# A bias of the attention scores: added by one-hot matmuls in TensorE instead of by a table spread through DRAM

## The reference

```
q, k, v, fz = split(h @ w_in)              # fz: one column for each head
q, k = rms_norm(q, q_g), rms_norm(k, k_g)  # per head
c = cumsum(log_sigmoid(fz + fgate_b))      # over the tokens, one row for each head
for i in range(2):                         # blocks of 128 queries
    logits = q_i @ k[:hi].T * 64 ** -0.5 + c[lo:hi, None] - c[None, :hi]
    probs = softmax(where(causal, logits, -inf))
    out_i = probs @ v[:hi]
x = x + out @ w_out
```

## Time and profile before

| | |
|---|---|
| median of 3 runs | 2485.47 us (2482.64 to 2490.33) |
| the profiled execution | 2485.47 us |
| its span | 2483.8 us |
| granted clock of TensorE, mean | 0.977 |
| busy: TensorE, VectorE, ScalarE, GpSimd | 95%, 66%, 47%, 40% |
| HBM read | 383.46 MB, 155 GB/s over the span |

### The profile page before, as it was taken

How to read it: one execution, slowest core, us unless ns; L and a number is a source line. 1 busy time by engine, 2 the same in 40 slices (tenths; PEclk the granted TensorE clock), 3 DMA queues, 4 the chain that set the end, 5 groups by cost and what they waited for, 6 DMA issues and landing times.

```text
span 2483.8 us, 51333 instructions
## 1 busy us (share of the span) xinstructions
PE 2363.2 (95%) x18282; PEld 2160.6 (87%) x18282; DVE 1642.6 (66%) x3051; ACT 1160.6 (47%) x1603; POOL 1003.5 (40%) x950
## 2 busy tenths in 40 slices
PE   6789998999999999998999989999999999889989
PEld 6779998999988888896899989998888888889987
DVE  5651899577788855435249967778886551334985
ACT  5434544333444455447444433334444454664444
POOL 5516797543333100014578854333320004654430
PEclk9889999999999999999999999999999999999999
DMA  4314555555555566643356545555556664444545
GB/s 144 104 41 139 160 180 155 164 160 160 159 167 165 167 191 193 193 144 111 106 158 184 180 145 158 163 161 162 168 162 185 194 194 131 129 127 135 169 152 152
DMA packets 108198, 385.72 MB, mean 155 GB/s; under 512 B 12464, under 2 KB 14800, under 8 KB 107728
## 3 DMA queue, kind: packets, MB, share of 16 engines
q1 hardware_dynamic: 104400, 379.13, 50.5%
q10 hardware_dynamic: 3712, 5.44, 0.7%
HBM read 383.46 MB, written 1.06 MB: 155 GB/s over the span
## 4 chain that ended last, share of the span: by engine, by line
PE 67%; POOL 12%; issue 10%; DVE 6%; ACT 2%; DVEq 1%; DMA 0%; POOLq 0%; ACTq 0%
POOL w_lo L366 12%; PE bank L1593 10%; PE bank L1595 10%; PE bank L1594 10%; PE bank L1504 9%; PE bank L1505 9%; PE bank L1507 9%; PE bank L1767 4%; DVE big L1416 2%; DVE big L1422 1%; DVE w_lo L871 1%; PE bank L1473 1%; DVE big L906 1%; PE bank L1510 0%; PE bank L1666 0%
## 5 line engine op out<-in xcount | busy, mean ns | idle before, releaser
L468 ACT ACTIVATE w_hi<-ring 128x1024 fp32r<-128x1024 f32 x719 | 758.3, 1057 | 793.1 <-PE bank L1595 422.7
L366 POOL TENSOR_TENSOR w_lo<-ring,w_hi 128x1024 fp32r<-128x1024 f32 x281 | 705.3, 2526 | 917.3 <-ACT w_hi L468 916.5
L1504 PE MATMUL bank<-x_hi,w_hi 128*128 128x256 f32 x3328 | 959.7, 289 | 40.3 <-ACT x_hi L481 16.8
L1505 PE MATMUL bank<-x_hi,w_lo 128*128 128x256 f32 x3328 | 947.0, 285 | 0.0
L1507 PE MATMUL bank<-x_lo,w_hi 128*128 128x256 f32 x3256 | 925.7, 284 | 0.0
L871 DVE TENSOR_TENSOR w_lo<-ring,w_hi 128x1024 fp32r<-128x1024 f32 x438 | 538.2, 1229 | 262.3 <-ACT w_hi L468 255.3
L1504 PEld LDWEIGHTS bank<-x_hi,w_hi 128*128 128x128 f32 x3328 | 645.5, 194 | 54.6 <-issue 24.8
L1505 PEld LDWEIGHTS bank<-x_hi,w_lo 128*128 128x128 f32 x3328 | 645.8, 194 | 0.0
L1507 PEld LDWEIGHTS bank<-x_lo,w_hi 128*128 128x128 f32 x3256 | 629.8, 193 | 0.0
L1593 PE MATMUL bank<-w_hi,x_hi 128*128 128x512 f32 x1112 | 440.4, 396 | 5.9 <-DVE x_lo L878 5.9
L1595 PE MATMUL bank<-w_lo,x_hi 128*128 128x512 f32 x1112 | 434.3, 391 | 0.0
(11 more groups left out here) (252 smaller groups left out, 2015.0 us busy)
## 6 DMA issues: line engine op xcount, KB each, us to landing
ring<-u_dram SPq DMA_DIRECT2D x256, 512.0 KB, 3.7
ring<-v_dram SPq DMA_DIRECT2D x256, 512.0 KB, 4.1
ring<-up_dram SPq DMA_DIRECT2D x44, 512.0 KB, 3.6
ring<-wq_dram SPq DMA_DIRECT2D x32, 512.0 KB, 3.7
ring<-sb_in_dram SPq DMA_DIRECT2D x31, 512.0 KB, 3.8
ring<-od_in_dram SPq DMA_DIRECT2D x25, 512.0 KB, 3.7
ring<-down_dram SPq DMA_DIRECT2D x22, 512.0 KB, 3.6
ring<-ev_in_dram SPq DMA_DIRECT2D x21, 512.0 KB, 3.8
```

Source lines behind the costliest of these rows:

```text
L366: pool.tensor_tensor(w_lo[:, k % RING, :], ring[:, k % RING, :], w_hi[:, k % RING, :].bitcast(F32), ALU.subtract).then_inc(g["lo_pool"], 1)
L468: A(w_hi[:, k % RING, :], ring[:, k % RING, :], ACT.Copy).then_inc(g["w_hi_done"], 1)
L1504: mm(dst, hi[:, rows[c]], xh[:, c, :], start=(c == 0), stop=False)
L1505: mm(dst, lo[:, rows[c]], xh[:, c, :], start=False, stop=False)
```

## The change

The write to DRAM, the spread, the table `fx_tab` and `mask_rows` are taken out. VectorE's masks read the plain causal mask. TensorE adds the bias in PSUM: after the two score matmuls of a block it runs two more that accumulate on them. Their weights are 16 rows of the identity's column `at + h`, repeated over 128 columns, and the moving operand is the 16 bias rows at partition `at` (0 or 64); the product is head h's bias row on all partitions. Before the loop TensorE waits for the bias rows. In VectorE, `head_norm` now runs over all eight blocks in one go, and the wait for the causal mask stands ahead of the loop.

```diff
@@ -175,7 +175,6 @@
         o_v = carve(TB * D)
         o_z = [carve(T) for _ in range(6)]
         causal = carve(3 * P)
-        fx_tab = carve(FH * 3 * P)
         fx_s, fx_p, fx_pt = ([carve(3 * P) for _ in range(4)] for _ in range(3))
         fx_max = carve(4 * 2)
         fx_sum, fx_inv = carve(2 * FH), carve(2 * FH)
@@ -220,8 +219,6 @@
         assert f_at + FC * T <= 27904
 
 
-        rows_dram = nc.dram_tensor("rows_dram", (FH, T), F32).ap()
-
         names = """x_loaded ev_tables_loaded tables_loaded keys_loaded od_tables_loaded sb_tables_loaded stored
             consts
             pieces_used units_out w_hi_done lo_pool lo_dve x_hi_done x_lo_done ax_hi ax_lo
@@ -233,7 +230,7 @@
             ev_chunk_sums ev_states ev_o ev_o_out ev_o_sq ev_o_sum ev_o_root ev_y
             conv_input conv_step taps_laid conv_mixed ln_sum ln_centred ln_sq ln_var ln_root ln_normed ev_ya
             od_z_in od_z_log od_bias_ready od_sq od_sum od_log od_root od_qk_ready od_sel
-            fox_rows_out fox_rows_spread fox_score fox_masked fox_exped fox_turned fox_pt_act fox_pt_dve fox_mixed fox_scaled fox_back
+            fox_score fox_masked fox_exped fox_turned fox_pt_act fox_pt_dve fox_mixed fox_scaled fox_back
             at_score at_masked at_exped at_prob at_turned at_pt at_mixed at_y
             sb_sq sb_sum sb_log sb_root sb_qk_ready sgu_mean sgu_root sgu_v_ready sgu_w_ready
             sgu_mixed sgu_y merged_out merged ff_silu ff_z ff_gated ff_tap""".split()
@@ -749,13 +746,6 @@
                 for s in SUM_GROUPS[j]:
                     A(o_sq[:, s * 512:(s + 1) * 512], o_qk[:, s * 512:(s + 1) * 512], ACT.Square).then_inc(g["od_sq"], 1)
                 unit(token_major(o_v, D, j), view=lambda s: b3(s, TB))
-                if j == 0:
-                    act.wait_ge(g["od_bias_ready"], 1)
-                    act.dma_start(rows_dram, o_z[5][0:FH, :]).then_inc(g["fox_rows_out"], 16)
-                if j == 1:
-                    act.wait_ge(g["fox_rows_out"], 16)
-                    act.dma_start(fx_tab.rearrange("p (h t) -> p h t", h=FH)[:, :, P:3 * P],
-                                  rows_dram.partition_broadcast(P)).then_inc(g["fox_rows_spread"], 16)
                 roots([(o_n[:, s * 512:(s + 1) * 512], bank[4 + s % 4][:, :]) for s in SUM_GROUPS[j]], HD,
                       "od_log", "od_root", 3 * j, "od_sum")
             highs(n[0] + 3)
@@ -1251,23 +1241,13 @@
                 settle()
                 V.tensor_tensor_scan(o_z[5], o_z[0], o_z[4], 0.0, ALU.mult, ALU.add).then_inc(g["od_bias_ready"], 1)
 
-            def mask_rows():
-
-                dve.wait_ge(g["od_sel"], 1)
-                dve.wait_ge(g["fox_rows_spread"], 16)
-                tab = fx_tab.rearrange("p (h c t) -> p h c t", h=FH, c=3)
-                below = causal[:, 0:P].rearrange("p (o t) -> p o t", o=1).to_broadcast([P, FH, P])
-                for dst, src in ((0, 1), (2, 2)):
-                    step(V.tensor_tensor(tab[:, :, dst], tab[:, :, src], below, ALU.add))
-
             def fox():
 
                 def mask(h):
                     S, top = fx_s[h % 4], fx_max[:, (h % 4) * 2:(h % 4) * 2 + 2]
-                    tab = fx_tab[:, h * 3 * P:(h + 1) * 3 * P]
                     dve.wait_ge(g["fox_score"], h + 1)
                     for b, cols in enumerate((slice(0, P), slice(P, 3 * P))):
-                        last = V.tensor_tensor_reduce(S[:, cols], bank[h % 4][:, cols], tab[:, cols], -1.0, -NEG_BIG,
+                        last = V.tensor_tensor_reduce(S[:, cols], bank[h % 4][:, cols], causal[:, cols], -1.0, -NEG_BIG,
                                                       ALU.add, ALU.min, top[:, b:b + 1])
                     last.then_inc(g["fox_masked"], 1)
 
@@ -1292,7 +1272,7 @@
                         V.tensor_tensor(x_lo[:, c], bank[(4, 0)[half] + j % 2][:, :], x_hi[:, c].bitcast(F32),
                                         ALU.subtract).then_inc(g["x_lo_done"], 1)
 
-                settle()
+                dve.wait_ge(g["od_sel"], 1)
                 for j in range(FH // 2):
                     mask(2 * j)
                     if j:
@@ -1306,9 +1286,9 @@
                 low_half(1)
                 xs[0] += 1
 
-            def head_norm(first, count, raw, dst, gain, root, ready):
-
-                for s in range(first, count):
+            def head_norm(count, raw, dst, gain, root, ready):
+
+                for s in range(count):
                     v = dst[:, s * 512:(s + 1) * 512]
                     dve.wait_ge(g[root], s + 1)
                     V.scalar_tensor_tensor(v, raw[:, s * 512:(s + 1) * 512], gain(s), v, ALU.mult, ALU.mult).then_inc(g[ready], 1)
@@ -1348,10 +1328,8 @@
             for k in range(12):
                 low(starts["od_in_b"] + k)
             log_sigmoid_rows()
-            of_qk = lambda s: qk_gain[:, 0:1] if s < 4 else qk_gain[:, 1:2]
-            head_norm(0, 6, o_qk, o_n, of_qk, "od_root", "od_qk_ready")
-            mask_rows()
-            head_norm(6, 8, o_qk, o_n, of_qk, "od_root", "od_qk_ready")
+            head_norm(8, o_qk, o_n, lambda s: qk_gain[:, 0:1] if s < 4 else qk_gain[:, 1:2],
+                      "od_root", "od_qk_ready")
             fox()
             u[0] += 13
             n[0] += 25
@@ -1363,7 +1341,7 @@
             norm(G_MIX2)
             step(V.tensor_scalar(nsink[:, :], sinks[:, :], -1.0, None, ALU.mult))
             dve.wait_ge(g["sb_tables_loaded"], 80)
-            head_norm(0, 3, s_qk, s_n, lambda s: qk_gain[:, 2:3] if s < 2 else qk_gain[:, 3:4],
+            head_norm(3, s_qk, s_n, lambda s: qk_gain[:, 2:3] if s < 2 else qk_gain[:, 3:4],
                       "sb_root", "sb_qk_ready")
             dve.wait_ge(g["units_out"], u[0] + 8)
             for tb in range(TB):
@@ -1832,8 +1810,12 @@
                     for lo, b, keys in ((0, 0, P), (P, 1, 2 * P)):
                         for h in (2 * j, 2 * j + 1):
                             at = 64 * (h % 2)
-                            last = mm(bank[h % 4][:, lo:lo + keys], qk[at:at + 64, j, b * P:(b + 1) * P],
-                                      qk[at:at + 64, 8 + j, 0:keys], start=True, stop=True)
+                            mm(bank[h % 4][:, lo:lo + keys], qk[at:at + 64, j, b * P:(b + 1) * P], qk[at:at + 64, 8 + j, 0:keys],
+                               start=True, stop=False)
+                        for h in (2 * j, 2 * j + 1):
+                            at = 64 * (h % 2)
+                            pick = ident[at:at + FH, at + h:at + h + 1].to_broadcast([FH, P])
+                            last = mm(bank[h % 4][:, lo:lo + keys], pick, o_z[5][at:at + FH, 0:keys], start=False, stop=True)
                             if b:
                                 last.then_inc(g["fox_score"], 1)
 
@@ -1897,6 +1879,7 @@
                 for s in SUM_GROUPS[j]:
                     pe.wait_ge(g["od_sq"], s + 1)
                     head_sums(s, o_sq, "od_sum", "od_log")
+            pe.wait_ge(g["od_bias_ready"], 1)
             pe.wait_ge(g["units_out"], u[0])
             fox()
             add_to_stream()
```

## The result

The changed kernel takes 2514.3 us (2510.2 to 2515.4, 5 runs) against 2485.5 (2482.6 to 2493.7, 5 runs): a ratio of 1.0102, with a 95% interval of 1.0088 to 1.0117. It is 29 us slower. Eight further runs of the changed kernel lie between 2506.3 and 2516.5. The forecast was 2487.7, with a range from 2481.5 to 2492.5. The profiled execution took 2516.4 us, with a mean clock of 0.965 against 0.977.

A forecast was written before the change was run, and what follows sets the result against it. TensorE was taken to bound the heads' loop, after waits caused by the table. Third scores 3.06 us earlier, rounds then 0.99 late, plus the last pair's 1.26, gave 2485.47 + 2.2 = 2487.7 us; range 2481.5 to 2492.5.

The forecast's parts named there:

- The removal: Ahead of the heads' loop: without table and additions, GpSimd's subtractions shorten, norms clear the way, first scores start 1.34 us earlier.
- The price of the picks: In the heads' loop on TensorE: four 16-row matmuls more per pair, 2.12 us against 0.86, so 1.26 more.
- Rounds of 4.34 on TensorE: Heads' loop, held by TensorE: five rounds of 3.06 + 1.26 = 4.32 us, 21.60 in all, where before they took 17.55.
- The sum: Whole stage: third scores 3.06 us earlier, five rounds end 0.99 late, last pair adds 1.26: 2.25 us slower.
- rival D: Heads' loop: whole wait gained, picks hidden behind ScalarE, about 6 us faster, 2479.5 us; chance 0.05.
- A: Pairs' scores in the heads' loop: picks overlap, 0.64 us more per pair, 2483.0 us; chance 0.24.
- E: Pairs' scores in the heads' loop: upper bound of the picks' price, 1.80 us more per pair, 2492 us; chance 0.09.
- the clock of the rounds: Heads' loop: the five rounds of 4.32 us were priced at the high clock, 1.00.
- rival C: Heads' loop: 16-row matmuls use little of the array, so the low clock holds throughout; up to 35 us more, 2523; chance 0.04.
- rival B: Start of the heads' loop: low clock stays as before or comes later, costing 3.5 us, 2491.2 us; chance 0.13.

The follow-up runs named there:

- e5_early_picks: The changed kernel with the 16-row picks left out for the last four pairs of heads and kept for the first four: 2494.2 us, ratio 1.0036.
- e6: The changed kernel with the 16-row picks left out for the first two pairs of heads alone: 2507.5 us, ratio 1.0078.
- e8: The changed kernel with 30 full-array filler matmuls put in ahead of the sixth pair's scores: 2507.1 us, ratio 1.0077.
- e11: The changed kernel with a pair's four scores put ahead of its four 16-row picks: 2509.2 us, ratio 1.0087.
- e1 to e4: The changed kernel with no picks (2483.8 us), 64-row picks (2482.2 us), 128-row picks (2492.0 us), no picks in the first four pairs (2479.2 us).
- e12: The changed kernel with picks of 64 rows instead of 16, run again in more rounds: 2487.0 us against 2487.3, ratio 0.9998.
- e4: The changed kernel with the picks of the first four pairs left out and the last four kept on 16 rows: 2479.2 us, one run.
- e7: The changed kernel with full-array filler matmuls, 4 ahead of the first scores, 8 behind each of the first two pairs: 2489.1 us, ratio 1.0018.

## Why the prediction was wrong

**What was right.** The removal, step by step: subtractions of 2.35 us, norms out of the way, first scores 1.40 us earlier (I had 1.34). The price of the picks at the high clock: 2.10 us a pair, where I had 2.12; the groups of 128 columns take 0.42 and those of 256 take 0.63, which is three slots each (0.32 and 0.64) with 0.10 and nothing on top, so the groups don't overlap. The Trainium skill's rule (TensorEngine Tiling (Array Packing), Key Properties), that a change of tiling mode drains the engine, agrees with that. The other side is this case's own: with 64-row picks, without a change, a pair takes 1.39 us. Rounds of 4.34 on TensorE, where I had 4.32. The sum: from the first scores to the transposes I had 1186.2 - 1147.4 = 38.8 us, and the filler kernel has 40.24 with 1.9 of filler in it. TensorE was the bound, so rival D is out (its terms add up to 6.65 and 2478.8, not 2479.5, and nothing hangs on that), and neither A nor E holds.

**The step that failed** is the clock of the rounds: the sum has five rounds at 3.06 + 1.26 = 4.32 us, and that holds only at 1.00. The other case stood in rival C. I gave it a chance of 0.04, and wrote against it that the loop of before "keeps 1.00 from 1162 to 1164 on 64 rows and narrow matmuls" and that the 16-row matmuls of the even layer ran at the high level too. Both readings are true (the trace has 1.00 from 39 to 41 us, too, which the earlier trace rows doesn't show), and both were read as if a level seen were a property of the work; the matmuls of the even layer were 1.1 us between two full-array ones. The rows that spoke to the question stood beside them: the loop of before had fallen to 0.50 at 1154 and had come back by about 1160.6. I priced that at 3.5 us, for 7 us at half speed (rival B), and did not ask what brought the clock back, though the change altered just the work that did it. Measured, a round takes 7.68 us at 0.50, and the stage 63.28 us instead of 38.8, so 24.5 us are the clock's.

**What the runs showed in its place.** From the fourth pair on, a loop with 16-row picks keeps the level that it has: 1.00 for four rounds behind a loop without picks, for the whole loop behind filler, for the last rounds behind a burst; 0.50 to the end otherwise. A loop without picks, or with picks of 64 or 128 rows, comes back from 0.50: 6.4 us after TensorE's start in the kernel before, 5.9 and 7.9 us with 64 and 128 rows, and 3.3 us after the first scores without picks in e5_early_picks. That is shown, each with one profile.

The fall comes in two ways. In the kernel before and in the two kernels with additions ahead of the masks it comes in a wait of 3.9 to 7.8 us. In five profiles (the changed kernel, e5, e6, e8 and e11) it comes without such a wait, and all five have 16-row picks within the first three pairs and no filler. In the five without such picks there and without a long wait (e1 to e4 and e12) it doesn't come. So rival C had the place, nearly the size (2523) and a part of the reason. What it had wrong is that 16 rows bring the low clock whatever came before: e4 and e7 run them at 1.00.

**What stays open** is why the clock falls within the early pairs and not within the rounds of e4_late_picks, where the same picks ran. In the changed kernel TensorE was busy from 1147.62 until past the fall, after a wait of 0.73 us. The Trainium skill (TensorE: Matmul & The Clock Gate, the section on oscillation in real kernels) tells of falls from idle gaps between bursts; the fall of the kernel before, in its wait of 3.91 us, agrees with that, and that of the changed kernel came behind a short wait with narrow matmuls running. With 64-row picks, the same short wait and three more of 0.59, 0.33 and 0.75 us, it did not fall in the two profiles. Open too is what of the 16 rows counts. It isn't that weights are zeros: the filler's all were, and so were all rows but one of the 64-row picks.

## What to carry to other kernels

When a trace shows a low clock that comes back by itself, the work that brings it back is a resource: ask of each change to that stretch whether it still would. Matmuls that use few rows cost more than their slots here, and rows with zero weights cost nothing: the one-hot operand on its neighbours' 64 rows took the same columns, saved 0.7 us a pair at the high clock (1.39 against 2.10), and let the clock return. On 128 rows it let the clock return too, but a pair took 2.76 us. A price worked out for one level of the clock should be written down for both, with the rows that say which one the stage will be granted. And a level seen in a row is a fact of that moment: before it is carried to other work, look at what stood ahead of it.

## What I had not expected of the hardware

The granted clock of one and the same round depends on what came before: 7.69 us at 0.50 and 4.35 us at 1.00 in one execution, with 30 filler matmuls (5.03 us) between the two kinds, though their weights were all zeros. And with TensorE busy 12.00 of 12.00 us the clock stayed at 0.50.
